# A hybrid decoder step on one core: state reads in column tiles, the decay on POOL, transposes and state steps in the second halves of chunks, head norms on quarters

## What is computed

```python
bcum = jnp.cumsum(gb, axis=2)
o = einsum('bhts,bhsv->bhtv', scores, ib) + einsum('bhtk,bhkv->bhtv', qb * exp(bcum), S)
S_new = exp(btot)[..., None] * S + einsum('bhsk,bhsv->bhkv', kdec, ib)
...
o = _rmsnorm(o, hg_norm_w)                 # per head, over 128 channels
o = o * silu(g)
merged = sigmoid(ga) * (a @ w_branch_a) + sigmoid(gb) * (o @ w_branch_b)
```

## Time and profile before

| what | us |
|---|---|
| median of three executions | 2158.28 |
| lowest, highest | 2157.68, 2161.81 |
| the profiled execution's own time | 2155.77 |
| its span (first to last instruction) | 2153.9 |
| TensorE busy | 2082.8 |
| VectorE busy | 1467.8 |
| ScalarE busy | 1142.4 |
| POOL busy | 98.0 |
| granted TensorE clock, mean | 0.984 of full |

### The profile page before, as it was taken

The page is one execution under the profiler, slowest core; times in us unless marked ns, Lnnn a source line. Parts: engine busy times, 40 slices in busy tenths (PEclk is TensorE's granted clock), DMA queues, the critical chain, the costliest instruction groups (busy, mean ns, idle before and its releaser), DMA issues. The chain is left out here.

```text
span 2153.9 us, 34595 instructions
## 1 busy us (share of the span) xinstructions
PE 2082.8 (97%) x13327; PEld 1860.8 (86%) x13327; DVE 1467.8 (68%) x1694; ACT 1142.4 (53%) x1149; POOL 98.0 (5%) x138
## 2 busy tenths in 40 slices
PE   7999999999999999999999899999999999999997
PEld 4999999888999889989889688888888888888885
DVE  4476555546344456745546588998989898988986
ACT  3433334344343443432424467686868777686864
POOL 2200001000000030000110100000000000000000
PEclk9999999999999999999999999999999999999998
DMA  9635465473666454435545489999999999999994
GB/s 320 211 106 154 142 192 156 156 227 118 203 208 218 135 164 141 123 103 171 169 155 186 172 278 382 327 403 325 395 338 373 363 344 387 323 405 327 398 338 186
DMA packets 244642, 528.77 MB, mean 245 GB/s; under 512 B 18200, under 2 KB 142218, under 8 KB 244531
## 3 DMA queue, kind: packets, MB, share of 16 engines
q1 hardware_dynamic: 234512, 496.56, 65.4%
q0 software_dynamic: 9648, 29.29, 4.4%
q10 hardware_dynamic: 370, 1.35, 0.2%
HBM read 514.54 MB, written 12.59 MB: 245 GB/s over the span
## 5 line engine op out<-in xcount | busy, mean ns | idle before, releaser
L1658 ACT ACTIVATE mhi<-mraw 128x2048 fp32r<-128x2048 f32 (+1 forms) x320 | 579.1, 1821 | 218.6 <-DMA mraw<-in_w_exp_up 84.2
L1128 DVE TENSOR_TENSOR mlo<-mraw,mhi 128x2048 fp32r<-128x2048 f32 (+1 forms) x319 | 680.6, 2163 | 8.6 <-ACT mhi L1658 8.2
L546 DVE TENSOR_TENSOR wlo<-raw,whi 128x1024 fp32r<-128x1024 f32 x244 | 289.4, 1212 | 322.6 <-ACT whi L1366 321.8
L1925 PE MATMUL ps<-h1h,whi 128*128 128x320 f32 x1248 | 395.0, 328 | 13.8 <-DVE h1l L1066 6.8
L1926 PE MATMUL ps<-h1l,whi 128*128 128x320 f32 x1248 | 374.5, 311 | 0.0
L2398 PE MATMUL ps<-mhi,xeh 128*128 128x512 f32 (+1 forms) x864 | 327.3, 379 | 2.1 <-DVE xel L1147 1.7
L2399 PE MATMUL ps<-mhi,xel 128*128 128x512 f32 (+1 forms) x864 | 321.8, 372 | 0.0
L1366 ACT ACTIVATE whi<-raw 128x1024 fp32r<-128x1024 f32 x244 | 248.0, 1046 | 121.4 <-PE ps L2297 44.8
L1925 PEld LDWEIGHTS ps<-h1h,whi 128*128 128x128 f32 x1248 | 237.9, 191 | 37.4 <-issue 30.9
L1926 PEld LDWEIGHTS ps<-h1l,whi 128*128 128x128 f32 x1248 | 238.2, 191 | 0.5 <-issue 0.5
L2404 PE MATMUL ps<-mlo,xeh 128*128 128x512 f32 (+1 forms) x864 | 225.0, 372 | 0.0
(11 more groups left out here) (390 smaller groups left out, 2724.6 us busy)
## 6 DMA issues: line engine op xcount, KB each, us to landing
mraw<-in_w_exp_down SPq DMA_DIRECT2D x198, 512.0 KB, 8.6
mraw<-in_w_exp_gate SPq DMA_DIRECT2D x154, 512.0 KB, 5.4
mraw<-in_w_exp_up SPq DMA_DIRECT2D x144, 512.0 KB, 6.5
raw<-in_w_in SPq DMA_DIRECT2D x128, 512.0 KB, 3.9
raw<-in_w_ada SPq DMA_DIRECT2D x72, 512.0 KB, 3.8
mraw<-in_w_exp_gate SPq DMA_DIRECT2D x72, 384.0 KB, 3.4
mraw<-in_w_exp_up SPq DMA_DIRECT2D x72, 384.0 KB, 4.0
pause<-in_w_ada SPq DMA_DIRECT2D x24, 512.0 KB, 5.2
```

Source lines behind the costliest of these rows:

```text
L546: V.tensor_tensor(WLO[:, u % RAW_UNITS, 0:w], RAW[:, u % RAW_UNITS, 0:w], WHI[:, h % HI_UNITS, 0:w].bitcast(F32), ALU.subtract).then_inc(l ...
L1128: V.tensor_tensor(MLO[:, n % RAW_RING, 0:w], MRAW[:, n % RAW_RING, 0:w], MHI[:, n % HI_RING, 0:w].bitcast(F32), ALU.subtract).then_inc(m_l ...
L1658: A.activation(MHI[:, n % HI_RING, 0:w], MRAW[:, n % RAW_RING, 0:w], ACT.Copy).then_inc(m_hi, 1)
L1925: M.matmul(out_, w, v[0], start=start, stop=False, skip_group_check=True)
```

## The change

Reads use the queries of four sequences (32 token columns) as weights and the state as the stream. Head h goes to the column tile h % 4 and to half h // 4 of the columns, so the result has token rows. VectorE copies it to `RD`, and a new ride, `back`, transposes its two halves; VectorE picks the 8 columns of the sequence and adds them. POOL multiplies the old state by its decay, in two halves, once the read's result has been copied (and so the read is over); VectorE's step is one addition of 4 x 128 columns, and waits for POOL. POOL's loads stand behind these multiplies. Backs and steps lie in slots 8 to 15, a step in one slot; steps 14 and 15 go behind gb3. The head norms are made in column tiles, a quarter of the columns to each group of 32 partitions, so that root (ScalarE, straight from PSUM, with scale and eps) and reciprocal run over 128 columns. A spread is four products with 128 rows, and the samples' norm has a spread of its own (`spread` 4, in gb3).

```diff
-         ("ga", 2): [(0, "o", 2), (4, "read", 0), (9, "norm", 2), (10, "step", 0), (12, "step", 1)],
-         ("ga", 3): [(0, "o", 3), (4, "read", 1), (9, "norm", 3), (10, "step", 2), (12, "step", 3)],
-         ("gb", 0): [(0, "read", 2), (4, "step", 4), (6, "step", 5), (8, "read", 3), (12, "step", 6), (14, "step", 7)],
...
-         ("gb", 3): [(1, "norm", 4), (6, "step", 14), (10, "step", 15)]}
+         ("ga", 2): [(0, "o", 2), (8, "read", 0), (9, "norm", 2), (11, "back", 0), (13, "step", 0), (15, "step", 1)],
+         ("ga", 3): [(0, "o", 3), (8, "read", 1), (11, "back", 1), (13, "step", 2), (15, "step", 3), (15, "norm", 3)],
+         ("gb", 0): [(0, "read", 2), (2, "read", 3), (8, "back", 2), (9, "back", 3),
+                     (10, "step", 4), (12, "step", 5), (14, "step", 6), (15, "step", 7)],
...
+         ("gb", 2): [(0, "read", 6), (2, "read", 7), (8, "back", 6), (9, "back", 7), (10, "spread", 0), (11, "spread", 1),
+                     (12, "step", 12), (13, "spread", 2), (14, "step", 13), (15, "spread", 3)],
+         ("gb", 3): [(2, "norm", 4), (8, "spread", 4)]}
-LASTS = {"o": 4, "within": 4, "read": 4, "step": 2, "norm": 1, "spread": 1}
+LASTS = {"o": 4, "within": 4, "read": 1, "back": 1, "step": 1, "norm": 1, "spread": 1}
# VectorE
-                dve.wait_ge(sq_used, nsq[0])
-                V.tensor_scalar(RST[0:rows, 0:n], PS[0:rows, 6, 0:n], 1.0 / size, EPS, ALU.mult, ALU.add)\
-                    .then_inc(ms_made, 1)
                 see.next(std_made)
-                see.step(V.reciprocal(RSTD[0:rows, 0:n], RST[0:rows, 0:n]), dve_step if rows == P else sem("heads_rstd"))
+                V.reciprocal(RSTD[:, 0:P], RST[:, 0:P]).then_inc(sem("heads_rstd"), 1)
...
                     elif what == "read":
                         b = aux()
+                        V.tensor_copy(RD[:, n % 2, :], PS[:, b, 0:2 * P]).then_inc(aux_out, 1)
+                        mark["rd", l, n] = x[0]
+                    elif what == "back":
+                        b = aux()
                         part = OS[:, :, n * LS:(n + 1) * LS]
-                        V.tensor_tensor(part, part, PS[:, b, 0:HEADS * LS].rearrange("p (h t) -> p h t", h=HEADS),
-                                        ALU.add).then_inc(aux_out, 1)
+                        back = PS[:, b, 0:2 * P].rearrange("p (h t) -> p h t", h=HEADS)
+                        V.tensor_tensor(part, part, back[:, :, n % 4 * LS:(n % 4 + 1) * LS], ALU.add).then_inc(aux_out, 1)
...
-                        for h in range(4 * (n % 2), 4 * (n % 2) + 4):
-                            ins = V.scalar_tensor_tensor(old[:, h, :], old[:, h, :], BS[:, h, s:s + 1],
-                                                         PS[:, b, (h % 4) * P:(h % 4 + 1) * P], ALU.mult, ALU.add)
-                        ins.then_inc(aux_out, 1)
+                        dve.wait_ge(sem("scaled"), 16 * l + n + 1)
+                        part = old[:, 4 * (n % 2):4 * (n % 2) + 4, :]
+                        V.tensor_tensor(part, part, PS[:, b, :].rearrange("p (h v) -> p h v", h=4), ALU.add)\
+                            .then_inc(aux_out, 1)
...
+                for n in (14, 15):
+                    ride("step", n)
                 after(c)
# POOL
                 for s in range(NS):
+                    t, place = state(s)
+                    pool.wait_ge(aux_out, mark["rd", l, s])
+                    pool.wait_ge(sem(f"st_in{place}"), 16 * (2 * l + s // 4 + 1))
+                    for g in range(2):
+                        part = t[:, 4 * g:4 * g + 4, :]
+                        pool.tensor_tensor(part, part, BS[:, 4 * g:4 * g + 4, s:s + 1].broadcast_to([P, 4, P]), ALU.mult)\
+                            .then_inc(sem("scaled"), 1)
                     if s + 3 < NS:
                         load_state(s + 3)
-                    t, place = state(s)
# TensorE
-                M.matmul(PS[0:4, 6, :], MARK[:, 3 - n:7 - n], OSQ[:, :], start=(n == 0), stop=(n == 3)).then_inc(sq_used, 1)
+                mark_ = MARK[:, 3 - n:35 - n] if n < 4 else ONES[:, 0:32]
+                for c in range(4):
+                    ins = M.matmul(PS[32 * c:32 * c + 32, 6, 0:P], mark_, OSQ[:, c * P:(c + 1) * P], start=(n % 4 == 0),
+                                   stop=(n >= 3), skip_group_check=True)
...
-                        for h in range(2 * at_, 2 * at_ + 2):
-                            ins = M.matmul(PS[:, b, h * LS:(h + 1) * LS], state(n)[0][:, h, :],
-                                           QQ[:, h, TP + n * LS:TP + (n + 1) * LS], start=True, stop=True)
+                        t0 = TP + 4 * LS * (n // 4)
+                        for h in range(HEADS):
+                            q = 32 * (h % 4)
+                            ins = M.matmul(PS[q:q + 32, b, h // 4 * P:(h // 4 + 1) * P], QQ[:, h, t0:t0 + 4 * LS],
+                                           state(n)[0][:, h, :], start=True, stop=True)
+                        read_at[n] = x[0]
+                    elif what == "back":
+                        for g in range(2):
+                            ins = M.transpose(PS[:, b, g * P:(g + 1) * P], RD[:, n % 2, g * P:(g + 1) * P], ident)
                     elif what == "spread":
-                        ins = M.matmul(PS[:, b, :], CF[0:4, C_ID + n:C_ID + n + 1].broadcast_to([4, P]), RSTD[0:4, :],
-                                       start=True, stop=True)
+                        for c in range(4):
+                            at_row = C_ID + 32 * c + n % 4
+                            ins = M.matmul(PS[:, b, c * P:(c + 1) * P], CF[:, at_row:at_row + 1].broadcast_to([P, P]),
+                                           RSTD[:, 0:P], start=True, stop=True)
...
+                for n in (14, 15):
+                    aux()
+                    pe.wait_ge(sem("im_made"), 16 * l + n + 1)
+                    for at_ in range(LASTS["step"]):
+                        ride("step", n, at_)
```

More of the change, by code:

```diff
@@ L590, in _, with heads_rstd @@
             nsq = [0]
[L592 removed]
+            def heads_rstd(tiles):
                 nsq[0] += tiles
[L595 to L597 removed]
                 see.next(std_made)
[L599 removed]
+                V.reciprocal(RSTD[:, 0:P], RST[:, 0:P]).then_inc(sem("heads_rstd"), 1)
             def rstd_dve(bank, lows=None):
@@ L1029, in ride @@
                         b = aux()
-                        for h in range(4 * (n % 2), 4 * (n % 2) + 4):
-                            ins = V.scalar_tensor_tensor(old[:, h, :], old[:, h, :], BS[:, h, s:s + 1],
-                                                         PS[:, b, (h % 4) * P:(h % 4 + 1) * P], ALU.mult, ALU.add)
-                        ins.then_inc(aux_out, 1)
+                        dve.wait_ge(sem("scaled"), 16 * l + n + 1)
+                        part = old[:, 4 * (n % 2):4 * (n % 2) + 4, :]
+                        V.tensor_tensor(part, part, PS[:, b, :].rearrange("p (h v) -> p h v", h=4), ALU.add)\
+                            .then_inc(aux_out, 1)
                         mark["st", l, n] = x[0]
+                    elif what == "spread" and n == 4:
+                        b = aux()
+                        h = HT[:, :, TP:T]
+                        V.tensor_tensor(h, OS[:, :, :], PS[:, b, :].rearrange("p (h t) -> p h t", h=HEADS), ALU.mult)\
+                            .then_inc(aux_out, 1)
+                        dve.wait_ge(aux_out, x[0])
+                        see.step(V.scalar_tensor_tensor(h, h, VEC[:, 1, 80 + l:81 + l], GS[:, :, TP:T],
+                                                        ALU.mult, ALU.mult), sem("on_made"))
                     elif what == "spread":
@@ L1387, in square, with root_heads @@
                 nsq[0] += 1
-            def root(n, rows=P):
-                see.next(ms_made)
-                A.activation(RST[0:rows, 0:n], RST[0:rows, 0:n], ACT.Sqrt).then_inc(std_made, 1)
+            def root_heads():
+                act.wait_ge(sq_used, nsq[0])
+                A.activation(RST[:, 0:P], PS[:, 6, 0:P], ACT.Sqrt, bias=EPST[:, 0:1], scale=1.0 / P).then_inc(std_made, 1)
             def root_quarters():
@@ L1589, in _ @@
                     if k == 3:
-                        root(512, 4)
+                        root_heads()
                     act.wait_ge(unit_used, ENDS[c])
@@ L1603, in _ @@
                     if k == 3:
-                        root(512)
+                        root_heads()
                     act.wait_ge(unit_used, ENDS[c])
@@ L1844, in aux, with stat @@
                 return 4 + (x[0] - 1) % 2
-            def stat(first, last, n=T, src=None):
+            def stat(first, last):
                 if first:
@@ L1853, in stat @@
                 pe.wait_ge(sq_made, counts["sq"])
-                if src is not None:
-                    ins = M.matmul(PS[:, 6, 0:n], ONES[:, :], src, start=first, stop=last)
-                else:
-                    for c in range(4):
-                        ins = M.matmul(PS[32 * c:32 * c + 32, 6, 0:TQ], ONES[:, 0:32],
```

(13 more changed lines are left out.)

25 lines of the change are left out of this document (11 added, 14 removed).

## The result

The changed kernel takes **2127.39 us** (median; 2122.71 to 2128.88), the kernel before beside it 2157.98 (2155.28 to 2161.81): a ratio of 0.9841, interval [0.9819, 0.9862]. The profiled execution went from 2155.77 to 2128.88 us (spans 2153.9 and 2127.0), 26.9 less. It is the slowest of the four of the kernel after, so the profile accounts for 27 of the 31 us.

A forecast was written before the change was run, and what follows sets the result against it. TensorE, busy 97% of the span, was taken as the bound. Per layer 12.3 us of work and 4.7 of waits go, 9.0 of new waits come: 8.0, two layers 16 us, so median 2142.3 us, range 2128 to 2152.

The forecast's parts named there:

- steps, 14 in one slot: TensorE's state steps: one slot with four products, 0.81 us instead of 0.88, saves a changeover; 1.0 us per layer.
- waits that go: TensorE's old waits in layer 0: 0.7 us for a freed bank, 0.6 masked row, 3.4 at B's start; 4.7 together.
- back 2: In gb0, the transpose of a read's copy waits 0.8 us, since VectorE copies only after the low halves.
- spread 4: In gb3, the samples' norm spread in slot 8 waits 2.4 us for the root and reciprocal.
- gap before B: Between gb3 and B: two steps, 1.5 us, then about 0.4 of wait; 1.9 us in all.
- low clock: Half-speed stretches per layer: three again, costing 5.0 us; the one in B goes, one in gb3 comes, no net gain.
- POOL's turn: POOL's queue cycle per state, store and load included: 7.6 us, so POOL falls behind TensorE by 1.4 us a turn.
- reads 5 to 7: In gb0 to gb2, TensorE waits for a state, a bank and a load: 0.9, 2.1 and 0.9 us.
- POOL keeps up: Rival, chance 0.25: stores land faster, POOL's cycle is some 6.2 us, 3.9 us and one half-speed stretch less per layer; 2131.
- third rival: Rival, chance 0.05: the reads' column tiles don't run side by side, a read costs 1.65 us; 2158, no change.
- POOL and VectorE in each other's way: Rival, 0.13 together with slower stores: POOL multiplies and VectorE low halves exclude each other, 2.4 us late, twice a layer; 2152.
- slow multiply: Rival, chance 0.04: the broadcast multiply on POOL is slow, at 4 us six turns wait 22 us per layer; 2178, slower.

## Why the prediction was right in direction and short in size

Layer 0's balance, forecast and measured, in us (gain positive):

| term | forecast | measured |
|---|---|---|
| reads, 8 | 5.8 | 6.2 |
| steps, 14 in one slot | 1.0 | 0 |
| steps 14 and 15 out of gb3 | 1.8 | 1.8 |
| norms, 5 | 3.0 | 3.2 |
| spreads | 0.7 | 0.35 |
| waits that go | 4.7 | 4.7 |
| back 2 | -0.8 | -0.4 |
| read 5 | -0.9 | 0 |
| read 6 | -2.1 | -0.9 |
| read 7 | -0.9 | -0.4 |
| spread 4 | -2.4 | -2.4 |
| gap before B | -1.9 | -2.0 |
| low clock | 0 | 3.3 |
| sum | 8.0 | 13.45 |

The stretch says 13.5. The low clock is a difference of two counts and not of waits: three falls before, one after. (Norms: 5 x (1.1 - 0.46). Spreads: 4 x (1.2 - 0.89) - 0.89. The other measured terms are from the starts and waits above.)

**The step that failed most is the count of low-clock stretches.** I wrote "three stretches again (gb0, gb2, gb3)". One came. The one in gb3 came as forecast, behind the 2.4 us wait. The one in gb0 was to follow a wait of 0.8 at back 2; the wait was 0.4, and the clock stayed. For the one in gb2 the forecast gave no reason; before, it stood behind four-row spreads, which the change itself takes away. Two stretches fewer are 3.3 us per layer, 6.7 of the 11 us that the profile gives more than forecast.

That they are gone is no accident of one execution: neither gb0 nor gb2 has a fall in either layer of the kernel after, of the run with spread 4 later, or of the five runs from the decay back on VectorE to the backs a slot later. (The doubled multiply brought one in gb2 of layer 1, behind a wait of its own.) Why they are gone stays open. The size of the wait does not settle gb0: with a wait of 1.8 us at back 2 the clock stayed full in both layers with the norms as before, and behind 1.9 at the same place it fell in both layers with the reads alone. Four-row spreads in gb2 were followed by a fall in layer 1 only in the former run, in layer 0 only in the latter.

**The second is POOL's turn.** I took 7.6 us, from stores of layer 1 that stand 6.7 us ahead of the next load. In gb0 and gb1 of the kernel after, a store stands 5.4 to 6.2 us ahead of it, and the turns are 6.5 to 7.1. Layer 0 of the kernel before, which the forecast did not use, had 5.3, 6.0 and 8.0 from store to load; the first of them:

```profile
356.23 0.89 POOL L1809 DMA_DIRECT2D out_ss<-stb  x1 [0.20 <-issue]
...
361.54 0.88 POOL L1796 DMA_DIRECT2D stb<-in_state_hgrn  x1 [4.42 <-DMA out_ss<-stb]
```

So the forecast took for fixed what varied by 2.7 us in the trace that it had. DMA issues of layer 0, of the kernel after from 358 to 384 (count, KB, median us to landing):

```profile
out_ss<-st POOLq DMA_DIRECT2D x2, 512.0 KB, 5.4
...
st<-in_state_hgrn POOLq DMA_DIRECT2D x2, 512.0 KB, 5.2
```

The same rows of the kernel before, from 355 to 385, give 6.5 and 5.7. The 5.8 of the earlier trace rows is over the whole stretch, and there the kernel after has 6.3, so its transfers are not faster throughout. Why those of gb0 and gb1 are, no run isolated. So reads 5 to 7 waited 1.3 us (0.3 in layer 1) in place of 3.9. These waits vary between runs of the same order: 1.1 and 1.3 with steps 14 and 15 back inside gb3, 0 and 0.4 with the root ahead. The rival "POOL keeps up" named this, with a turn of 6.2 and 2131 us. Its price counted 5.5 per layer: 3.9 of waits and one low clock. Both low clocks that stayed away carry the result past it. The forecast's order within the turn (load, store, two multiplies, wait) is the one the timeline shows.

**The median.** The profiled execution was forecast at 2139.8 and took 2128.88, 10.9 less. The other 4.0 us of the 14.9 by which the median missed are the step from the profile to the median: I added 2.5, and the median lies 1.5 below its profile. No mechanism stands behind that.

**Smaller misses.** A step in one slot costs 0.88, as two rides did: the changeover that I counted away (14 x 0.07) isn't saved. A read costs 0.77 where I took 0.65, its back 0.22 where I took 0.38; the errors cancel. The multiply took 1.03 us for 1.2.

**What held.** The reads' tiles lie side by side: 16 records in 0.64 us, far from the 1.65 of the third rival. Spread 4 waits 2.4 us, to the tenth: root at 397.24 and the quarter reciprocal of 0.95 end at 398.7, and the spread starts at 398.81. The gap before B is 2.0 us for the 1.9 forecast, but not as forecast: its 16 records take all of it and no wait is behind them, where 1.5 us of steps and 0.4 of wait were counted.

The rival of POOL and VectorE in each other's way has a real mechanism, shown in the run with the multiplies doubled, but in this kernel they miss each other, as the prediction's times had it. The slow multiply was excluded by its 1.03 us, and doubling it cost 8.3 us, not the whole gain.

By removal from the changed kernel, the parts are worth 14.5 us (reads), 11.2 (norms and spreads), 1.3 within the noise (steps out of gb3) and none (the decay on POOL). They are no exact sum: a low clock more or less came with several of these runs, and back 2 waits longer without the quarters.

## What to carry to other kernels

Two f32 products of 8 columns cost 0.44 us of TensorE here, as much as two of 128, and one of 512 columns was 1.12 us with 4 rows and 1.02 with 128; turning a read round, so that the small side is the weights in column tiles, paid 0.77 us even with a copy and transposes behind. When a change takes away idle time and thin work behind which the granted clock fell, give each low-clock stretch of before its own question, whether what stood ahead of it is still there, and let the range reach to the case where none comes; even with the same wait in place it came in some runs here and not in others. After such a change look for the one wait that is left: moving spread 4 and a root by a few slots gave another 10 us, a third of it the low clock that stayed away.

## What was not expected of the hardware

- The granted clock falls without a wait: behind eight 8-column rides in gb1 of layer 0 (window 372 to 378 at 0.72, TensorE busy throughout) and in gb0 of layer 1 (0.72 from 1068 to 1074), and not behind the other four groups of eight.
- The same instructions and waits do not always make it fall: with four-row spreads in gb2 the granted clock was 1.00 from 392 to 400 in layer 0, and 0.72 from 1096 to 1102 in layer 1. It also stayed at full behind waits of 0.9, 1.5, 1.8 and 2.4 us in one run or another, where a fall followed the 0.7 in gb0 of the kernel before. Most falls lasted about 3.5 us, two of them 6.8. What decides was not settled, so a forecast should give each fall a chance and not a count.
- A 128x512 f32 multiply with a broadcast operand takes 1.03 us on POOL, no more than the 613 ns cast made likely; an overlap with VectorE's two-tile subtraction brings it to 1.9 to 2.0.
- A median lies up to 4.4 us from the profiled execution of the same kernel, in either direction (2120.29 and 2115.89 with spread 4 later, 2126.41 and 2130.66 with the decay on VectorE): an effect of 2 us per layer needs the stretches beside the medians.
